# Turns and products of the second and third inverse level, issued in alternation

## The reference, cut to what matters

```python
def gated_delta_rule_chunked(q, k, v, g, beta):
    ...
    lower = jnp.where(strict, jnp.einsum('bhncd,bhnsd->bhncs', kb, k) * decay, 0.0)
    a_mat = lower + jnp.eye(c, dtype=jnp.float32)
    rhs = jnp.concatenate([vb, kb * jnp.exp(gc)[..., None]], axis=-1)
    sol = lax.linalg.triangular_solve(a_mat, rhs, left_side=True, lower=True,
                                      unit_diagonal=True)
```

## Time and profile before

| | |
|---|---|
| median of 3 runs | 1164.46 us (1163.23 to 1164.78) |
| the profiled execution | 1164.17 us |
| its span, first to last instruction | 1162.5 us |
| TensorE busy | 1137.6 us (98%) |
| VectorE busy | 529.6 us (46%) |
| ScalarE busy | 455.0 us (39%) |
| GpSimd busy | 552.3 us (48%) |
| mean granted TensorE clock | 0.998 of full speed |
| the four chunks, roughly | 165 to 420 us of the span |

### The profile page before, as it was taken

The page is one execution under the profiler, slowest core; times in us unless marked ns, Lnnn a source line. Parts: engine busy times, 40 slices in busy tenths (PEclk is TensorE's granted clock), DMA queues, the critical chain, the costliest instruction groups (busy, mean ns, idle before and its releaser), DMA issues.

```text
span 1162.5 us, 16609 instructions
## 1 busy us (share of the span) xinstructions
PE 1137.6 (98%) x5981; PEld 946.9 (81%) x5981; DVE 529.6 (46%) x1133; ACT 455.0 (39%) x744; POOL 552.3 (48%) x298
## 2 busy tenths in 40 slices
PE   6999999999999999999999999999999999999997
PEld 5878888888888878888888888887888888888886
DVE  5343446464738256777777662613333333330001
ACT  6354353434344345555555432234222322322112
POOL 6334456362626145656665644434444444444443
PEclk9999999999999999999999999999999999999999
DMA  6323333231313233333333273532333333322231
GB/s 194 85 77 106 90 96 99 71 91 55 100 56 93 72 109 84 97 90 92 89 99 99 73 231 99 159 91 74 107 92 91 107 91 92 107 91 91 91 109 72
DMA packets 169632, 113.61 MB, mean 98 GB/s; under 512 B 6257, under 2 KB 157922, under 8 KB 169586
## 3 DMA queue, kind: packets, MB, share of 16 engines
q1 hardware_dynamic: 163218, 98.26, 29.6%
q10 hardware_dynamic: 6368, 14.72, 3.5%
HBM read 104.54 MB, written 8.42 MB: 97 GB/s over the span
## 4 chain that ended last, share of the span: by engine, by line
PE 86%; DVE 6%; issue 4%; POOL 2%; ACT 1%; DMA 0%; SPq 0%; DVEq 0%; ACTq 0%; POOLq 0%
PE ps L1427 61%; PE ps L1839 10%; PE ps L1516 6%; PE ps L1409 4%; PE ps L1732 2%; POOL w_lo L559 1%; PE ps L1699 1%; PE ps L1700 1%; DVE ps L1161 1%; DVE prod L1171 1%; DVE Wb L1176 1%; PE ps L1775 1%; PE ps L1471 1%; DMA prm_rows<-in_gdn_norm_w 0%; POOL rn L554 0%
## 5 line engine op out<-in xcount | busy, mean ns | idle before, releaser
L559 POOL TENSOR_TENSOR w_lo<-raw,w_hi 128x1024 fp32r<-128x1024 f32 x170 | 417.1, 2454 | 522.5 <-ACT w_hi L686 522.5
L1427 PE MATMUL ps<-h_hi,w_hi 128*128 128x512 f32 x976 | 385.1, 395 | 1.0 <-POOL w_lo L559 1.0
L1427 PE MATMUL ps<-h_hi,w_lo 128*128 128x512 f32 x976 | 384.7, 394 | 0.0
L1427 PE MATMUL ps<-h_lo,w_hi 128*128 128x512 f32 x976 | 383.7, 393 | 0.0
L686 ACT ACTIVATE w_hi<-raw 128x1024 fp32r<-128x1024 f32 x170 | 180.2, 1060 | 466.4 <-PE ps L1427 367.2
L1427 PEld LDWEIGHTS ps<-h_hi,w_hi 128*128 128x128 f32 x976 | 183.8, 188 | 39.7 <-issue 1.9
L1427 PEld LDWEIGHTS ps<-h_hi,w_lo 128*128 128x128 f32 x976 | 183.8, 188 | 37.3 <-issue 0.2
L1427 PEld LDWEIGHTS ps<-h_lo,w_hi 128*128 128x128 f32 x976 | 183.7, 188 | 36.0
L1041 DVE SCALAR_TENSOR_TENSOR tmp<-ps,prm,tmp 128x511 f32<-128x511 f32 (+2 forms) x72 | 53.9, 748 | 82.0 <-ACT tmp L716 76.8
L652 POOL TENSOR_SCALAR probs<-probs,rsum 128x128 f32<-128x128 f32 (+1 forms) x64 | 70.2, 1114 | 17.8 <-DVE rsum L1266 16.9
L1009 DVE TENSOR_SCALAR ms<-ss 128x1 f32<-128x1 f32 x8 | 1.2, 154 | 125.7 <-ACT raw L982 117.4
(11 more groups left out here) (260 smaller groups left out, 1570.6 us busy)
## 6 DMA issues: line engine op xcount, KB each, us to landing
raw<-in_w_in SPq DMA_DIRECT2D x80, 512.0 KB, 3.9
raw<-in_w_gate SPq DMA_DIRECT2D x22, 512.0 KB, 3.8
raw<-in_w_up SPq DMA_DIRECT2D x22, 512.0 KB, 3.8
raw<-in_w_down SPq DMA_DIRECT2D x22, 512.0 KB, 3.3
gate_dram<-gate ACTq DMA_DIRECT2D x24, 256.0 KB, 2.0
cumb<-cum_dram ACTq DMA_DIRECT2D x8, 512.0 KB, 3.5
raw<-in_w_branch_a SPq DMA_DIRECT2D x8, 512.0 KB, 3.8
raw<-in_w_branch_b SPq DMA_DIRECT2D x8, 512.0 KB, 3.9
```

The lines of the kernel that those rows point to most:

```text
L559: pool.tensor_tensor(w_lo[:, r % 2, :], raw[:, r, :], w_hi[:, r % 2, :], ALU.subtract)\
L1427: return pe.matmul(ps[:, bank, :], wts[wl][k], acts[xl][:, k, :], start=(n == 0), stop=(n == len(PASSES) - 1))
```

## The change

The two kinds are issued in alternation. In the second level, head by head, the order is now turn of pair 0, product of pair 0, turn of pair 1, product of pair 1. In the third level it is turn, product for each head. The instructions, their operands, banks and semaphores are the same, and each semaphore is still raised by the last instruction of its half. In the second level all four raises now come with the last head.

```diff
@@ -1606,12 +1606,14 @@
                 pe.wait_ge(Zd_added, c * 4 + 2)
-                for r in range(2):
-                    pair(r, lambda m, left, right: pe.transpose(pair_bank(4 + r)[:, m, :], Zm[left, m, left],
-                                                                ident[left, left]), T_turned)
-                for r in range(2):
-                    pair(r, lambda m, left, right: mm(pair_bank(2 + r)[:, m, :], L[right, m, left],
-                                                      Zm[right, m, right]), Y_done)
+                for m in range(H):
+                    for r, (left, right) in enumerate(PAIRS):
+                        turned = pe.transpose(pair_bank(4 + r)[:, m, :], Zm[left, m, left], ident[left, left])
+                        if m == H - 1:
+                            turned.then_inc(T_turned, 1)
+                        below = mm(pair_bank(2 + r)[:, m, :], L[right, m, left], Zm[right, m, right])
+                        if m == H - 1:
+                            below.then_inc(Y_done, 1)
                 fill(FILLS[4])
...
@@ -1620,11 +1622,13 @@
                 fill(FILLS[5])
                 pe.wait_ge(Zd_added, c * 4 + 4)
-                for a in range(2):
-                    per_head(a, lambda h, m: turn(bank4(4 + a)[0:64, h, 0:64], Zm[0:64, m, 0:64]), T_turned)
-                for a in range(2):
-                    per_head(a, lambda h, n: mm(half_bank(2 + a)[0:64, h, :], L[64:P, n, 0:64], Zm[64:P, n, 64:P]),
-                             Y_done)
+                for m in range(H):
+                    a, h = m // 4, m % 4
+                    turned = turn(bank4(4 + a)[0:64, h, 0:64], Zm[0:64, m, 0:64])
+                    below = mm(half_bank(2 + a)[0:64, h, :], L[64:P, m, 0:64], Zm[64:P, m, 64:P])
+                    if h == 3:
+                        turned.then_inc(T_turned, 1)
+                        below.then_inc(Y_done, 1)
                 fill(FILLS[6])
```

## The result

| | before | after |
|---|---|---|
| median | 1164.26 us | 1219.12 us |
| range | 1163.23 to 1164.78 | 1218.3 to 1220.44 |
| the profiled execution | 1164.17 us | 1220.44 us |
| its span | 1162.5 us | 1218.8 us |
| mean granted TensorE clock | 0.998 | 0.963 |

Time after over time before is 1.0472, 95% interval 1.0459 to 1.0484. The change costs 54.9 us. The prediction had the direction and the price of the alternation at full clock, 20.6 us. Its sum had no term for the clock, and the other 34.3 us are there.

A forecast was written before the change was run, and what follows sets the result against it. TensorE, busy 98% of the span, was taken as the bound. Per chunk +3.15 (second level), +1.64 (third) and +0.36 (cold turns) make 5.15 us, 20.6 for four; 1164.17 + 20.6 = 1184.8 us, range 1173 to 1194.

The forecast's parts named there:

- both places are on the path and nothing absorbs them: Both rewritten stages lie on TensorE's chain; its three waits for `Zm`, 2.6 us together, do not absorb the added time.
- a change between turn and product empties the array though the row groups differ: In second and third levels, each change of kind drains TensorE, the first product coming some 0.09 us late.
- The price at full clock: Alternated second and third levels with a drain at every change of kind: +5.15 us per chunk, 20.6 us for four.
- the copies stay covered: VectorE's and ScalarE's copies after each stage finish behind fills before needed; if not in the third level, 0.25 us a chunk.
- The rival of half the drains: Only turn to product waits, product to turn follows at once: +10.5 us over four chunks, 1174.7 us; 12%.
- No effect: Kinds overlap a little and drain a little, leaving the time within 2.3 us of before; 5%.
- all drains at full clock: Every change of kind in both levels drains the array while the clock holds: 1184.8 us, own range 1181 to 1188; 50%.
- A fall was a rival with 25%: Drains plus TensorE's clock falling to 0.50 once per chunk, 7.0 us more in all: 1191.8 us; 25%.
- The size of a fall: In the clock case, each chunk's fall costs 1.76 us, taken from one stretch of 3.42 us at half clock.

The follow-up runs named there:

- matmul_turns: Alternates both levels like the changed kernel, but each turn is an ordinary two-pass matmul with the identity instead of transpose mode; 1159.75 us, 0.9961 of the kernel before.
- small_longer: Kernel before with the second level's first products made five times over, same operands and place, a single change of kind; 1204.04 us, ratio 1.0333.
- chunk0_only: Both levels alternate as in the changed kernel, but only in the first of four chunks, the others as before; 1178.99 us, 1.0115 of the kernel before.
- spread_fills: Changed kernel's alternation with two fills behind every second head, 12 a chunk, taken from the chunk's end; 1241.79 us, 1.0667 of the kernel before.
- matmul_grouped: Kernel before with turns made by ordinary matmuls with the identity, all still ahead of the products; 1168.51 us, ratio 1.0028.
- same_kind: Kernel before, transpose mode and one change of kind kept, second level's two pairs alternating head by head within each kind; 1163.14 us, ratio 0.9992.

## Why the prediction was right and wrong, point by point

- That both places are on the path and nothing absorbs them: right. TensorE's waits are the same, and the cost stands in its busy time.
- That a change between turn and product empties the array though the row groups differ: right. In `matmul_turns` the same alternation without transpose mode overlaps, and the earlier trace rows show that transpose mode over the whole array makes no step.
- The price at full clock: right. The forecast was 4.64 + 0.16 = 4.80 us for the second level, and 4.86 was measured; 3.28 + 0.20 = 3.48 for the third, and 3.43 was measured. Together +5.15 per chunk was forecast and +5.16 measured. That it fits to the hundredth is luck: the two misses cancel. The step from product to turn, which no row before showed, is 0.13 us in the second level, as the step to a fill.
- That the copies stay covered: right. VectorE's last copy ended at 208.53, the second product started at 210.44.
- The rival of half the drains: refuted by the same rows. No effect: refuted.
- The clock: this is the step that failed. The sum ran all drains at full clock, at 50%, and so put the clock at nothing. A fall was a rival with 25%, "against it: the array is never idle for more than some 0.1 us". But idleness is not needed for a fall: in `small_longer` the clock falls while TensorE works without a gap. In the changed kernel it fell in every chunk, 85.3 us at half clock, and this is 34.3 of the 54.9 us.
- The size of a fall: mis-sized in the rival too. It took 1.76 us per fall, from the only fall in the trace before, 3.42 us long. Here a fall lasts 20.48 us and costs 8.4 (`chunk0_only`). 4 x 5.16 + 4 x 8.4 = 54.2 us, measured 54.9. The fall of the earlier trace rows had large fills behind it, those of the chunks have small pieces until the third level is over. The row was read for its length without asking what TensorE did in it, and with this size the range could not reach the result.

Open: what about the small pieces brings the clock down, whether it is they that keep it there, why two falls of 10.24 us ended earlier, and what would have held the clock in `spread_fills`.

## What to carry to other kernels

In these runs, row groups of TensorE work side by side only while the array's division stays the same. Before interleaving two kinds of small matmuls, look at the step between the last of one kind and the first of the other: if it is 0.1 us longer than within a kind, every alternation pays it. Transposes in transpose mode and products of the same size can differ in this, and an ordinary matmul with the identity removed it here. And a stage of small matmuls that was stretched from 1.49 to 4.86 us cost 8.4 us more in clock behind it, so when such a stage gets longer, its price at full clock is a lower bound. Before taking the price of a slow stretch from one place of a trace, look at what the engine did in it there, and what it will do in the new place.

## What the runs showed of the hardware that I had not expected

- A fall of TensorE's clock from 2.4 to 1.2 GHz lasted 6.83 to 30.72 us in the chunks, 20.48 us in 8 of 20 cases. Fills of 128x512 start 0.43 us apart in it in place of 0.23. Each us of it cost 0.40 to 0.41 us (34.3 us for 85.3 in the changed kernel, 8.4 for 20.48 in `chunk0_only`).
- In 18 of the 20 the clock came back 2.7 to 5.6 us after the last small product of the third level. The falls behind the chunks, where no such small products stand, lasted 3.41 us (before, changed kernel and others) or 6.83 us (`chunk0_only`, `matmul_grouped`).
- In the changed kernel it came 2.9 to 5.2 us after the start of the alternated second level. In `small_longer` it came 3.2 to 5.1 us after the start of the stage, though TensorE worked without a gap.
- Alternating row groups within one kind brings passes of 32x32 products from 0.03 us apart to less than 0.02 (32 passes in 0.50 us, `same_kind`).
